# Weaving the first layer's attention with its projection, and taking slabs into the delta stage

## The chip, the cores and the metric

The kernel runs on one core of one Trainium2 chip. It is a single launch that holds its whole activation state in SBUF and streams all weights from HBM. The metric is the device time of that core in microseconds (us): the kernel before takes 2646.89 us, the median of three runs (2643.5 to 2648.5).

## The reference

Two transformer blocks run one after the other on 512 tokens of width 1024, all in fp32:

```python
def reference(...):
    x = first_block(x, mem, ...)        # two layers
    return second_block(x, meta, ...)   # two layers, 16 meta tokens ahead: 528 tokens

# first_block, layer i
h = rmsnorm(x, norm_mix[i]); mkv = rmsnorm(mem) @ w_mem_kv[i]
# i = 0: 12 query heads on 4 key heads, window of 128 either side, ALiBi bias, sink logit
# i = 1: 12 heads, neighbourhood of 8 x 16 on a grid of width 64, learned bias
y_tok = windowed_gqa(...) if i == 0 else neighbourhood_attn(...)
y_mem = memory_attn(qm, mk, mv)         # 4 heads, dense on 256 memory tokens, no bias
x = x + concat(y_tok, y_mem) @ w_out[i]
x = x + (silu(g) * u) @ w_down[i]       # g, u = rmsnorm(x) @ w_gate_up[i]

# second_block, layer 0: even_mixer
a_gate_in, a_gate_out, a_h, qkv, z, beta, alpha = split(h @ w_in)
y_a = a_gate_out * causal_dwconv(a_gate_in * a_h)
q, k, v = split(silu(causal_dwconv(qkv)))       # q and k are l2-normed, 4 heads of 128
o = gated_delta_rule(q, k, v, sigmoid(beta), g(alpha))   # chunks; state 128 x 128 a head
y_b = rms_norm(o, dn_norm_w) * silu(z)          # by head, over its 128 features
x = x + concat(y_a, y_b) @ w_out
# then a convolutional FFN; layer 1: sliding-window attention with sinks, and its FFN
```

## The kernel before

**Numbers and weights.** An fp32 product is made of three: each operand is split into a rounded half "hi" and the rest "lo", and TensorE adds hi x hi, hi x lo and lo x hi. Activations lie with features on the partitions, eight tiles of 128 features by 528 tokens. Weights come as slabs of 128 output features with all 1024 inputs (`UP`). A ring of two slots s = 0, 1 holds them: SyncE loads `raw` when GpSimd has ended the split before (`load_slabs`, `stream`), ScalarE rounds it to `w_hi` in two halves of 512 columns (`split_hi`, L987), GpSimd makes `w_lo` (`split_lo`, L695), TensorE multiplies (`many`, L1466: 24 products for 512 tokens, 48 where 528 tokens are taken as two times 264), and VectorE evicts PSUM and frees slot and accumulator (`acc_free[s]`). The pair q of slots is counted through the whole program.

**The order.** `plan()` lists the stages. Every engine walks them with its own in-order program; semaphores tie the five programs together. Nothing is reordered at run time, so an instruction that waits holds up all behind it on its engine.

**First layer.** `proj(10, 2, 1)` makes all twelve slabs (eight of queries, two of keys, two of values) before its attention. The attention goes by pairs: one block of 128 queries of two heads. There are 24 window pairs (six tiles of two heads, four blocks, 256 keys at the edges and 384 inside) and eight memory pairs. For a pair TensorE makes scores (L1591), VectorE adds the bias and takes maxima (L2013, L2008), ScalarE the exponentials, TensorE turns the probabilities (L1604), ScalarE copies them back, TensorE multiplies the values (L1660) and spreads the inverse sums (L1675), ScalarE and VectorE keep and normalise (`spread`, `move_y`, `invert`, `normalise`); GpSimd splits queries, keys and outputs. Eight output slabs (`out`) follow.

**Second layer.** Its attention is woven already: `proj(2, 6, 1)`, and then one list of 32 pairs, eight of memory and 24 of the neighbourhood (`woven_row`). On TensorE each pair's turn is

```python
scores(p)
if p.back(2).exists:
    transpose(p.back(2))
woven_part(p)
if p.back(3).exists:
    values(p.back(3))
```

with `woven_part` half a slab (L1694): six pairs of slabs, query and key tile of two heads, in rows 0 to 23, and from row 24 on output tiles by `OUT_PARTS`. An entry (s, k) there is slab s, feature tile k; a half of a slab's tiles needs that half of its split. GpSimd's `attend_woven` interleaves `prepare` (the splits of queries, keys and values and the bias mask, four "chores" a pair of heads) with the half splits and the outputs' splits; before its first chore it waits for both accumulators of the projection.

**Even stage.** 28 slabs; the last four make the gate that multiplies the convolved branch `conv_y`, evicted on VectorE at the end of `even`. While they run, ScalarE and VectorE end the l2 norms and the gates of the delta rule.

**Delta stage.** Chunks of 16, 128, 128, 128 and 128 tokens go through a software pipeline: rounds -1 to 5 of six pieces each (`rounds`, `PIECES`). In a round one chunk is prepared (`new`, `pre`), one has its triangular matrix inverted by up to six levels of doubling (`here`, `first_product` L1830 and `second_products`, with masked matrices `a_lv` from GpSimd, L917), and one runs through the state (`old`, `tail`: value of the keys, turned keys, new values, output, state; `tail` 0 to 4). `gated_split` on GpSimd splits the gated branch tile by tile in rounds 1 to 4. After the last round `tile_norm` normalises the four heads over all 528 tokens (squares on ScalarE, sums by products with ones L1811, root, VectorE, rounding L1359, GpSimd's `head_split` L910). Only then do the eight output slabs begin: TensorE waits for `gated_lo` and `head_lo`.

Of the kernel before, what the change touches and what calls it, by code (L numbers as in the profile page):

```python
# [17 lines left out]
P = 128  # L18
# [62 lines left out]
def plan():  # L81
# [84 lines left out]
    slabs(28, UP)  # L166
# [3 lines left out]
    add("tn", what="head", n=4)  # L170
    c["tn"] += 4
# [22 lines left out]
def delta_steps():  # L194
# [7 lines left out]

    for c, (_, n) in enumerate(CHUNKS):
# [4 lines left out]
        for part, engines in (("pre", pre), ("tail", tail)):  # L208
# [14 lines left out]
def build(nc, d):  # L223
# [6 lines left out]
    with ctx:  # L230
# [125 lines left out]
        neg_ident = small("neg_ident", [P, P])  # L356
        dn_cst = small("dn_cst", [P, d["dn_consts"].shape[1]], f32, 12416)
# [50 lines left out]
        split_acc = acc(2, 2)  # L408

# [112 lines left out]

        class Pair:
# [63 lines left out]
        def woven_rest(st):  # L587
# [4 lines left out]
        OUT_PARTS = {24: [(0, 6), (0, 7)], 25: [(0, 0), (0, 1)], 26: [(0, 2)], 27: [(1, 6), (1, 7)], 28: [(1, 0)],  # L592
                     29: [(1, 1)], 30: [(1, 2)], 31: [(0, 3)]}
# [12 lines left out]
        def _(sp):  # L606
# [50 lines left out]
            for n, st in enumerate(stages):  # L657
# [9 lines left out]
                if st.kind == "att" and st.woven:  # L667
# [4 lines left out]
                    for i in range(st.nt):  # L672
                        stream(st.slab0 + 4 + 2 * i)
                        if i + 2 < st.nt:
                            load_bias(st, i + 2)
# [13 lines left out]
        def _(pool):  # L689
# [27 lines left out]
            def prepare(st):  # L717
# [26 lines left out]
                def stage_k(i):  # L744
# [15 lines left out]
                    elif st.woven:  # L760
                        src, kt = ring_tiles(st, i)[1], t
# [50 lines left out]
            def attend_woven(a):  # L812
# [4 lines left out]
                for s in range(RING):  # L817
                    pool.wait_ge(acc_free[s], first)
# [4 lines left out]
                for p in row:  # L823
                    u, n = p.at // 4, p.at % 4
                    if p.at + 4 < len(row):
                        then = row[p.at + 4]
                        if then.st is b and n < 2:
                            pool.wait_ge(acc_free[n], first + then.tile + 1)
                        chores[then.st][n](then.tile)
                    if n < 2 and 1 <= u <= W_TILES:  # L830
                        split_lo(first + u, 1, UP, (n,))
                    if n >= 2 and u < W_TILES:
                        split_lo(first + u + 1, 0, UP, (n - 2,))
# [4 lines left out]
                streamed(2 * (first + W_TILES) + 2)  # L838
# [59 lines left out]
            def gated_split(st, m):  # L898

                for s in range(RING):  # L900
                    pool.wait_ge(acc_free[s], st.slab0 // 2)
# [5 lines left out]
            def head_split(st):  # L907
                for j in range(4):
                    pool.wait_ge(head_hi, j + 1)
                    nc.gpsimd.tensor_tensor(h_lo[st.h][:, 4 + j, :], normed_o[:, j % 2, :],  # L910
                                            h_hi[st.h][:, 4 + j, :].bitcast(f32), ALU.subtract).then_inc(head_lo, 1)

            def delta(st):

                pool.wait_ge(loaded, 16 * N_LOADS + 16)
# [6 lines left out]
                for here, mid, old, new, i in rounds():  # L922
# [33 lines left out]
                stream(st.slab0 + 2)  # L956

            for n, st in enumerate(stages):
# [3 lines left out]
                if st.kind == "tn" and st.what == "head":  # L962
                    head_split(st)
# [13 lines left out]
        def _(act):  # L977
# [98 lines left out]
            def attend(st):  # L1076
                off = 1 if st.sink is None else 0

                def probs(p, h):
# [3 lines left out]
                    s_h = s_sb[0:p.nq, p.slot, h, off:p.n + 1]  # L1083
# [56 lines left out]
                def spread(p):  # L1140

                    if st.summed:
                        return
                    act.wait_ge(inv_ready, p.kept + 1)
# [6 lines left out]
                def move_y(p):  # L1151
                    if st.summed:
# [39 lines left out]
                def turned_woven(p):  # L1192
                    act.wait_ge(pt_done, 2 * p.count + 2)
                    act.wait_ge(pv_done, p.count - 1)
# [3 lines left out]
                def split_woven(p):  # L1198
                    first, u, n = st.slab0 // 2, p.at // 4, p.at % 4
                    if n < 2 and 1 <= u <= W_TILES:  # L1200
                        split_hi(first + u, 1, UP, (n,))
                    if n >= 2 and u < W_TILES:
# [1447 lines left out]
```

## Time and profile before

| | us |
|---|---|
| median of three runs | 2646.89 |
| the profiled execution, its own time | 2646.34 |
| its span from first to last instruction | 2644.6 |
| TensorE busy in the span | 2541.5 |
| TensorE loading weights | 2196.2 |
| GpSimd / VectorE / ScalarE busy | 1201.3 / 959.7 / 919.9 |
| mean granted TensorE clock, of full speed | 0.981 |

Times in the trace count from the start of the span. A line Lnnn is a line of the kernel; helpers share one line, so a group is told apart by its tiles (`w_lo<-raw,w_hi`). A duration of a group "x12" runs from the first instruction to the end of the last. Idle time in brackets stands before the instruction, with what ended it. The granted clock is the mean over a stretch: 1.0 is 2.4 GHz, 0.5 is 1.2 GHz.

### The profile page before, as it was taken

What the parts mean: (1) busy time and instruction counts of PE and PEld (TensorE: products, weight loads), DVE (VectorE), ACT (ScalarE), POOL (GpSimd) and SP (SyncE); (2) the same over time, 40 slices, a digit from 0 to 9 for tenths busy, and PEclk for the clock granted to TensorE, in tenths of its full rate; (3) what the DMA queues carried; (4) which work ended last, traced back from release to release, by engine and by line L of the source; (5) the groups of instructions that cost most, each with busy time, mean ns of one, the idle gap of its engine ahead of it and who ended that gap; (6) DMA issues with size and microseconds to landing.
All of it is one profiled execution on the core that took longest, in us unless ns stands there. A gap on an engine that the chain in (4) does not pass through costs nothing.

```text
span 2644.6 us, 46681 instructions
## 1 busy us (share of the span) xinstructions
PE 2541.5 (96%) x16758; PEld 2196.2 (83%) x16758; DVE 959.7 (36%) x1748; ACT 919.9 (35%) x1988; POOL 1201.3 (45%) x1039
## 2 busy tenths in 40 slices
PE   7999999999999999999998979999999888999999
PEld 7767888888776888888997869999999667998897
DVE  4263221223445221226753433422432543441341
ACT  4284322232244322234242223322233565322231
POOL 4554444444565444444442534444444443444443
PEclk9999999999999999999998989999999999999999
DMA  5211232232121222232221002232222100223222
GB/s 174 80 42 64 95 103 87 91 106 83 53 63 58 92 95 99 87 107 88 83 77 41 2 20 93 87 101 78 92 93 75 33 25 33 90 93 99 92 93 97
DMA packets 59473, 209.16 MB, mean 79 GB/s; under 512 B 8544, under 2 KB 11232, under 8 KB 59360
## 3 DMA queue, kind: packets, MB, share of 16 engines
q1 hardware_dynamic: 59360, 207.66, 24.1%
q8 instruction: 70, 1.15, 0.2%
q14 instruction: 43, 0.35, 0.0%
HBM read 205.54 MB, written 2.10 MB: 79 GB/s over the span
## 4 chain that ended last, share of the span: by engine, by line
PE 90%; DVE 4%; ACT 2%; issue 2%; POOL 1%; SPq 1%; DVEq 0%; DMA 0%; ACTq 0%; POOLq 0%
PE ps L1466 74%; PE ps L1694 3%; PE ps L1660 2%; PE ps L1642 1%; PE ps L1830 1%; PE ps L1591 1%; PE ps L1619 1%; PE ps L1819 1%; DVE s_sb L2013 1%; PE ps L1481 1%; PE ps L1669 1%; PE ps L1684 1%; DVE y_sb L1988 0%; DVE s_sb L1988 0%; PE ps L1604 0%
## 5 line engine op out<-in xcount | busy, mean ns | idle before, releaser
L695 POOL TENSOR_TENSOR w_lo<-raw,w_hi 128x512 fp32r<-128x512 f32 (+1 forms) x704 | 977.4, 1409 | 1156.1 <-ACT w_hi L987 1155.7
L987 ACT ACTIVATE w_hi<-raw 128x512 fp32r<-128x512 f32 (+1 forms) x704 | 428.2, 653 | 1276.0 <-PE ps L1466 1256.5
L1466 PE MATMUL ps<-h_hi,w_hi 128*128 128x264 f32 (+2 forms) x2832 | 791.4, 329 | 11.4 <-POOL h_lo L910 8.0
L1466 PE MATMUL ps<-h_lo,w_hi 128*128 128x264 f32 (+2 forms) x2832 | 789.5, 328 | 0.0
L1466 PE MATMUL ps<-h_hi,w_lo 128*128 128x264 f32 (+2 forms) x2832 | 786.8, 328 | 0.0
L1466 PEld LDWEIGHTS ps<-h_hi,w_hi 128*128 128x128 f32 x2832 | 479.8, 189 | 64.9 <-issue 13.8
L1466 PEld LDWEIGHTS ps<-h_lo,w_hi 128*128 128x128 f32 x2832 | 476.5, 189 | 48.1 <-issue 1.0
L1466 PEld LDWEIGHTS ps<-h_hi,w_lo 128*128 128x128 f32 x2832 | 476.7, 189 | 47.2
L1466 PE MATMUL ps<-act_lo,w_hi 128*128 128x512 f32 (+1 forms) x880 | 280.5, 351 | 0.0
L1466 PE MATMUL ps<-act_hi,w_lo 128*128 128x512 f32 (+1 forms) x880 | 279.8, 350 | 0.0
L1466 PE MATMUL ps<-act_hi,w_hi 128*128 128x512 f32 (+1 forms) x880 | 278.8, 349 | 0.0
L1988 DVE TENSOR_TENSOR x<-x,ps 128x512 f32<-128x512 f32 (+3 forms) x96 | 66.6, 693 | 432.0 <-PE ps L1466 430.5
L1466 PEld LDWEIGHTS ps<-act_hi,w_hi 128*128 128x128 f32 x880 | 153.3, 188 | 24.4
L1466 PEld LDWEIGHTS ps<-act_lo,w_hi 128*128 128x128 f32 x880 | 153.6, 188 | 24.0
L1466 PEld LDWEIGHTS ps<-act_hi,w_lo 128*128 128x128 f32 x880 | 153.9, 188 | 22.7
L1988 DVE TENSOR_TENSOR ps<-gated,ps 128x512 f32<-128x512 f32 (+1 forms) x88 | 61.6, 701 | 169.4 <-PE ps L1466 169.1
L1983 DVE SCALAR_TENSOR_TENSOR ps<-padded,vec,ps 128x528 f32<-128x528 f32 (+1 forms) x132 | 101.2, 767 | 25.9 <-issue 15.5
L1988 DVE TENSOR_TENSOR act_lo<-ps,act_hi 128x512 f32 (+1 forms) x88 | 61.2, 696 | 104.3 <-ACT act_hi L1252 104.3
L1988 DVE TENSOR_TENSOR padded<-ps,rstd 128x528 f32<-128x528 f32 (+1 forms) x56 | 39.4, 703 | 154.8 <-PE ps L1466 143.6
L1983 DVE SCALAR_TENSOR_TENSOR h_lo<-x,vec,h_hi 128x512 fp32r<-128x512 f32 (+2 forms) x64 | 59.4, 928 | 81.2 <-ACT h_hi L994 68.1
L1249 ACT ACTIVATE ps<-ps 128x512 f32<-128x512 f32 (+1 forms) x88 | 51.5, 585 | 105.8 <-DVE ps L1983 105.8
L1988 DVE TENSOR_TENSOR gated<-ps,rstd 128x512 f32<-128x512 f32 (+1 forms) x88 | 61.2, 696 | 73.2 <-ACT ps L1249 73.2
(311 smaller groups left out, 2785.0 us busy)
## 6 DMA issues: line engine op xcount, KB each, us to landing
raw<-slabs_d SPq DMA_DIRECT2D x288, 512.0 KB, 3.3
raw<-slabs_d SPq DMA_DIRECT2D x64, 704.0 KB, 4.0
bias_sb<-alibi_d SPq DMA_DIRECT2D x6, 384.0 KB, 3.7
x<-x_d SPq DMA_DIRECT2D x1, 2048.0 KB, 13.5
out_d<-x SPq DMA_DIRECT2D x8, 256.0 KB, 4.4
rpb_raw<-rpb_d SPq DMA_DIRECT2D x6, 256.0 KB, 2.7
mem_in<-mem_d SPq DMA_DIRECT2D x1, 1024.0 KB, 7.2
cst<-consts_d SPq DMA_DIRECT2D x1, 792.0 KB, 9.4
```

What stands on the lines that cost most here:

```text
L695: nc.gpsimd.tensor_tensor(w_lo[:, s, a * P:b * P], raw[:, s, a * P:b * P], w_hi[:, s, a * P:b * P].bitcast(f32), ALU.subtract).then_inc(lo ...
L987: nc.scalar.activation(w_hi[:, s, a * P:b * P], raw[:, s, a * P:b * P], ACT.Copy)\
L1249: nc.scalar.activation(acc(2, st.used), acc(2, st.used), ACT.Silu).then_inc(silu_ready, 1)
L1466: last = nc.tensor.matmul(ps[:, s * 2 * BANK + po:s * 2 * BANK + po + n], w[:, s, wk], columns(a, k, to, n), start=(k == 0 and w is w_hi a ...
L1481: last = nc.tensor.matmul(out, a[:, k, t0:t0 + n], w[:, s, wk], start=(k == 0 and w is w_hi and a is hi), stop=(k == DT - 1 and w is w_lo))
L1591: last = nc.tensor.matmul(p.score(h)[0:p.nq, col:col + n], a[hp, p.tile_slot, p.q], b[hp, p.tile_slot, k0:k0 + n], start=(b is k_hi and a ...
L1619: last = nc.tensor.transpose(to, s_sb[0:p.nq, p.slot, h, 1 + col:1 + col + n], ident[0:p.nq, 0:p.nq])
L1642: last = nc.tensor.matmul(split_acc[:, c, :], wt[:, w.s, k * P:(k + 1) * P], a[:, k, to:to + n], start=(k == 0 and wt is w_hi and a is hi) ...
L1660: nc.tensor.matmul(out[HD * h:HD * h + HD, 0:p.nq], v_st[0:n, p.tile_slot, vb, HD * h:HD * h + HD], p_t[0:n, p.slot, h, j, 0:p.nq], start= ...
L1694: last = nc.tensor.matmul(acc(s, 1), w[:, s, k * P:(k + 1) * P], columns(a, k, META, SEQ), start=(k == first and w is w_hi and a is hi), s ...
L1983: return nc.vector.scalar_tensor_tensor(*a, **kw)
L1988: return nc.vector.tensor_tensor(*a, **kw)
```

## The change

Three stages take part. **First layer:** it is woven as the second. Its projection keeps two memory query slabs and two value slabs; the memory pairs come first; eight slabs stand in the list: two key-and-query pairs in halves (rows 0 to 7), then, since three query heads share a key head, four query slabs in quarters (rows 8 to 23), all of them in one accumulator; the other accumulator serves the turned probabilities of window pairs, which need a bank more. Output tiles stand in rows 24 to 31 (`OUT_FIRST`). `spread`, `move_y` and `invert` join the woven lists of ScalarE and VectorE.

**Shared by both woven layers:** GpSimd's chores begin when the first accumulator is free, and the second layer's output tiles go in the order 0, 1, 2, 6, 7 with two rows between the slab's halves.

**Delta stage:** the four gate slabs leave the even stage for pieces 0 to 11 of the delta stage, a third of a slab each (`GATE_PARTS`), with their splits in pieces 3 to 13 (`GATE_SPLITS`), which also split the first halves and second halves of two output slabs. The head norm goes chunk by chunk two rounds behind (`mean_o`, `square_o`, `root_o`, `norm_o`, `head_round`, `head_split`). The last chunk's turned keys and state update go (`ends`). Quarters and halves of the first two output slabs are put into the last round and behind it (`out_part`). The host lays the first layer's weights out in the new order.

```diff
-    proj(10, 2, 1)
-    out[-1].queries = (0, 1, 2, 4)
+    proj(2, 2, 1)
+    out[-1].queries = (0,)
+    out[-1].woven = True
+    att(nt=2, blocks=m_blocks, bias=None, sink=None, qt=0, kt=0, group=1, y=6, layer=0)
+    out[-1].woven = True
+    slabs(2 * 2, UP)
     att(nt=6, blocks=a_blocks, bias="alibi", sink=0, qt=0, kt=6, group=3, y=0, layer=0)
-    att(nt=2, blocks=m_blocks, bias=None, sink=None, qt=8, kt=0, group=1, y=6, layer=0)
-    tail(2, 1, 0, False, (3, 1))
+    out[-1].woven = True
+    slabs(4, UP)
+    tail(2, 1, 0, False, (3, 1), woven=True)
...
-    slabs(28, UP)
+    slabs(24, UP)
     add("delta", pre=norms[-1])
-    add("tn", what="head", n=4)
+    slabs(4, UP)
...
+    ends = dict(pe=["vks", "vn", "o"], dve=["res"], act=["vn", "o"], pool=["ke", "qe"])
...
+        GATE_PARTS, GATE_SPLITS = 12, {3: (1, 0, 0), 4: (1, 0, 1), 6: (1, 1, 0), 7: (1, 1, 1), 9: (2, 0, 0),
+                                       10: (2, 0, 1), 12: (2, 1, 0), 13: (2, 1, 1)}
...
-        OUT_PARTS = {24: [(0, 6), (0, 7)], 25: [(0, 0), (0, 1)], 26: [(0, 2)], 27: [(1, 6), (1, 7)], 28: [(1, 0)],
-                     29: [(1, 1)], 30: [(1, 2)], 31: [(0, 3)]}
+        OUT_FIRST = {24: [(0, 0)], 25: [(0, 1)], 26: [(0, 2)], 27: [(0, 6)], 28: [(0, 7)], 31: [(0, 3)]}
+        def woven_slab(a, p):
+            first, u, n = a.slab0 // 2, p.at // 4, p.at % 4
+            if u >= W_TILES:
+                return None
+            if u < 2 or not shares_keys(a):
+                return first + u, n // 2, range(n % 2 * DT // 2, (n % 2 + 1) * DT // 2), n // 2
+            return first + 2 + (u - 2) // 2, u % 2, range(n * DT // 4, (n + 1) * DT // 4), 0
...
+        OUT_PARTS = {24: [(0, 0), (0, 1)], 25: [(0, 2)], 26: [(0, 6), (0, 7)], 27: [(1, 0), (1, 1)], 28: [(1, 2)],
+                     29: [(1, 6)], 30: [(1, 7)], 31: [(0, 3)]}
...
-                for s in range(RING):
-                    pool.wait_ge(acc_free[s], first)
+                pool.wait_ge(acc_free[0], first)
                 for n in (0, 1, 2):
                     chores[a][n](0)
...
+                        if then.st is a and n == 0:
+                            pool.wait_ge(acc_free[1], first)
...
+                    if e in GATE_SPLITS:
+                        pair, s, part = GATE_SPLITS[e]
+                        split_lo(st.slab0 // 2 + pair, s, UP, (part,))
+                    if past_o and i == 5:
+                        head_split(st, past_o)
...
                         probs(p, 1)
+                        if p.back(1).exists:
+                            spread(p.back(1))
+                        if p.back(2).exists:
+                            move_y(p.back(2))
                         if p.back(3).exists:
                             y_hi(p.back(3))
                         split_woven(p)
...
+                def gate_part(t):
+                    m, part = divmod(t, 3)
+                    q, s = st.slab0 // 2 + m // 2, m % 2
+                    if part == 0:
+                        begin(q, s)
+                        pe.wait_ge(acc_free[1 - s], q + s)
...
-                for here, _, old, new, i in rounds():
+                for here, _, old, new, i, e, past_o in parts():
+                    if e < GATE_PARTS:
+                        gate_part(e)
                     if here:
                         first_product(here, here.levels[i])
...
+                    if past_o and i == 1:
+                        mean_o(past_o)
+                    if old and old.c == LAST.c and i == 2:
+                        LAST.after(pe, "pre", "dve", "qk")
+                        LAST.after(pe, "pre", "act", "off")
+                        out_part(0, range(0, 2))
+                out_part(0, range(2, 4))
+                mean_o(LAST)
+                LAST.after(pe, "tail", "act", "o")
+                out_part(1, range(0, 4))
+                for s in range(RING):
+                    out_part(s, range(4, DT))
```

## Rows read from the trace of the kernel before

**Rows 1.** The page, parts 1 and 4: busy time by engine, chain by engine.
```profile
PE 2541.5 (96%) x16758; PEld 2196.2 (83%) x16758; DVE 959.7 (36%) x1748; ACT 919.9 (35%) x1988; POOL 1201.3 (45%) x1039
...
PE 90%; DVE 4%; ACT 2%; issue 2%; POOL 1%; SPq 1%; DVEq 0%; DMA 0%; ACTq 0%; POOLq 0%
```

**Rows 2.** Windows: length, PE, PEld, DVE, ACT, POOL busy, clock, DMA, GB/s.
```profile
121.38:209.57 88.19, 78.45 (x736) 55.69 (x737) 60.48 (x193) 70.61 (x257) 44.66 (x69) 0.94 0.11 34
1423.00:1445.26 22.26, 11.90 (x124) 10.30 (x124) 8.24 (x25) 7.12 (x20) 6.80 (x15) 0.61 0.00 1
1445.26:1470.50 25.24, 22.75 (x338) 19.42 (x339) 10.65 (x23) 7.20 (x18) 12.14 (x14) 0.91 0.01 2
1470.50:1541.20 70.70, 61.84 (x984) 55.58 (x985) 31.41 (x62) 18.76 (x45) 34.91 (x37) 0.93 0.02 7
1541.20:1572.48 31.28, 15.31 (x69) 12.66 (x69) 11.04 (x13) 10.94 (x18) 5.69 (x5) 0.72 0.07 21
```

**Rows 3.** Chain of waits, first layer: start, us, what (eight and nine slabs).
```profile
76.06 44.52 PE ps L1466 x192
...
209.57 51.73 PE ps L1466 x216
```

**Rows 4.** Chain of waits, second layer, woven rows.
```profile
677.74 5.49 PE ps L1694 x12
...
739.84 0.59 PE ps L1660 x8
740.42 0.44 PE ps L1669 x8
...
742.00 2.78 PE ps L1694 x12
```

**Rows 5.** Timeline of TensorE, first layer: start, us, operation.
```profile
150.08 0.91 PE L1604 MATMUL ps<-cst,s_sb 128*128 128x128 f32 x6
...
152.70 0.65 PE L1604 MATMUL ps<-cst,s_sb 128*128 128x128 f32 x4
```

**Rows 6.** Timeline of VectorE and GpSimd, start of the second layer's woven list.
```profile
672.99 1.27 DVE L1998 COPY val_w<-ps 128x384 f32<-128x384 f32 x3
...
673.02 0.61 POOL L723 CAST q_hi<-ring 128x512 fp32r<-128x512 f32 x1 [9.73 <-issue]
```

**Rows 7.** Timeline of GpSimd and TensorE, second layer, row 24 and end.
```profile
800.84 1.26 POOL L695 TENSOR_TENSOR w_lo<-raw,w_hi 128x512 fp32r<-128x512 f32 x1 [0.37 <-ACT w_hi L987]
...
802.36 0.70 PE L1694 MATMUL ps<-y_w,w_hi 128*128 128x512 f32 x2 [3.41 <-POOL w_lo L695]
...
841.50 0.73 PE L1466 MATMUL ps<-y_w,w_hi 128*128 128x512 f32 x2 [1.43 <-POOL w_lo L695]
```

**Rows 8.** Chain of waits, the four gate slabs of the even stage.
```profile
1399.46 23.47 PE ps L1466 x192
```

**Rows 9.** Timeline of VectorE, ScalarE and TensorE, start of the delta stage.
```profile
1404.48 0.18 DVE L1983 SCALAR_TENSOR_TENSOR gate<-dn_s,ea 128x20 f32<-128x20 f32 x1 [0.44 <-issue]
...
1423.01 1.15 ACT L987 ACTIVATE w_hi<-raw 128x512 fp32r<-128x512 f32 x2 [4.72 <-PE ps L1466]
...
1445.26 1.12 PE L1830 MATMUL ps<-x_m,a_lv 64*64 64x64 f32 x16 [3.16 <-POOL a_lv L917]
```

**Rows 10.** Timeline of four engines, end of the delta stage.
```profile
1545.77 1.89 PE L1819 MATMUL ps<-res,x_full 128*128 128x128 f32 x8
...
1564.47 0.70 ACT L1352 ACTIVATE root<-ps,vec 128x528 f32<-128x528 f32 x1 [1.06 <-PE ps L1811]
...
1568.07 1.34 POOL L910 TENSOR_TENSOR h_lo<-normed_o,h_hi 128x528 fp32r<-128x528 f32 x1 [6.72 <-ACT h_hi L1359]
...
1586.97 0.70 DVE L1988 TENSOR_TENSOR x<-x,ps 128x528 f32<-128x528 f32 x1 [2.43 <-PE ps L1466]
```

**Rows 11.** Timeline of VectorE: the state's update in two rounds.
```profile
1493.96 0.96 DVE L1988 TENSOR_TENSOR state<-state,erow 128x512 f32<-128x512 f32 x1
...
1550.43 0.69 DVE L1988 TENSOR_TENSOR state<-state,erow 128x512 f32<-128x512 f32 x1 [3.87 <-PE ps L1891]
```

More of the change, by code:

```diff
@@ L207, in delta_steps @@
                    pool=["em", "xm", "first", "xt"])
-        for part, engines in (("pre", pre), ("tail", tail)):
+        for part, engines in (("pre", pre), ("tail", tail if c + 1 < len(CHUNKS) else ends)):
             for engine, names in engines.items():
@@ L356, in build @@
         neg_ident = small("neg_ident", [P, P])
+        o_sq = small("o_sq", four)
         dn_cst = small("dn_cst", [P, d["dn_consts"].shape[1]], f32, 12416)
@@ L521, in rounds, with parts @@
                     yield here, mid, old, new, i
+        def parts():
+            for e, (here, mid, old, new, i) in enumerate(rounds()):
+                r = e // PIECES - 1
+                yield here, mid, old, new, i, e, Chunk(r - 2) if r >= 2 else None
+        GATE_PARTS, GATE_SPLITS = 12, {3: (1, 0, 0), 4: (1, 0, 1), 6: (1, 1, 0), 7: (1, 1, 1), 9: (2, 0, 0),
+                                       10: (2, 0, 1), 12: (2, 1, 0), 13: (2, 1, 1)}
+        LAST = Chunk(len(CHUNKS) - 1)
         class Pair:
@@ L826, in attend_woven @@
                         then = row[p.at + 4]
+                        if then.st is a and n == 0:
+                            pool.wait_ge(acc_free[1], first)
                         if then.st is b and n < 2:
-                            pool.wait_ge(acc_free[n], first + then.tile + 1)
+                            if then.tile < 2 or not shares_keys(a):
+                                pool.wait_ge(acc_free[n], first + then.tile + 1)
+                            elif n == 0:
+                                pool.wait_ge(acc_free[then.tile % 2], first + 2 + (then.tile - 2) // 2 + 1)
                         chores[then.st][n](then.tile)
[L830 to L833, printed above, removed]
+                    for q, s, part in woven_splits(a, p):
+                        split_lo(q, s, UP, (part,))
                     if p.back(3).exists:
@@ L920, in all_heads @@
                     return m[0:n, 0:w].unsqueeze(1).to_broadcast([n, DN_H, w])
-                for here, mid, old, new, i in rounds():
+                for here, mid, old, new, i, e, past_o in parts():
                     if here:
@@ L1140, in spread @@
                 def spread(p):
-                    if st.summed:
+                    if p.st.summed:
                         return
+                    if p.row and p.back(2).exists and p.back(2).st.summed:
+                        act.wait_ge(y_ready, p.count - 1)
                     act.wait_ge(inv_ready, p.kept + 1)
@@ L1198, in split_woven @@
                 def split_woven(p):
[L1199 to L1202, printed above, removed]
-                        split_hi(first + u + 1, 0, UP, (n - 2,))
+                    for q, s, part in woven_splits(st, p):
+                        split_hi(q, s, UP, (part,))
                 if st.woven:
@@ L1215, in attend @@
                     turned_woven(last)
-                    for k in (2, 1, 0):
-                        y_hi(last.back(k))
+                    spread(last)
+                    move_y(last.back(1))
+                    y_hi(last.back(2))
+                    move_y(last)
+                    y_hi(last.back(1))
+                    y_hi(last)
                     return
@@ L1418, in delta @@
                         pre(new, i)
+                    if e in GATE_SPLITS:
+                        pair, s, part = GATE_SPLITS[e]
+                        split_hi(st.slab0 // 2 + pair, s, UP, (part,))
+                    if past_o and i == 0:
+                        square_o(past_o)
+                    if past_o and i == 2:
+                        root_o(past_o)
+                    if past_o and i == 4:
+                        head_round(past_o)
+                square_o(LAST)
+                root_o(LAST)
+                head_round(LAST)
             for st in stages:
@@ L1841, in first_product @@
                     k.after(pe, "levels", "pool", ("am", s))
+                    if s == k.levels[0] and k.c == 0:
+                        pe.wait_ge(gate_made, 2)
                     if s == k.levels[0]:
@@ L1920, in delta @@
                     pe.wait_ge(acc_free[s], st.slab0 // 2)
-                for here, _, old, new, i in rounds():
+                for here, _, old, new, i, e, past_o in parts():
+                    if e < GATE_PARTS:
+                        gate_part(e)
                     if here:
@@ L2503, in delta @@
                     fill(x_fulls[e][SIDE:P, :, 0:SIDE], 0.0).then_inc(gate_made, 1)
-                for here, _, old, new, i in rounds():
+                for here, _, old, new, i, e, past_o in parts():
                     if here:
```

236 lines of the change are left out of this document (169 added, 67 removed).

## The prediction

> **What bounds the kernel now.** I read the page's first and fourth parts, then stages by windows, then chain and timeline around each edit. TensorE is busy for 2541.5 of 2644.6 us and holds 90% of the chain that ended last [rows 1]. A gain must therefore come from the few stretches where TensorE waits or works at the lower of its two clocks: the attention of the first layer (78.45 us busy in 88.19), the first two rounds of the delta stage (11.90 in 22.26, mean granted clock 0.61) and its end with the norm of the heads (15.31 in 31.28) [rows 2].
>
> **Terms.** The profiled execution took 2646.34 us (span 2644.6); the median of the runs is 2646.89, so a difference found in the trace is taken from 2646.5. I follow three stretches from one fixed point to another, and call a saving negative.
>
> **A, first layer: from the end of its fourth slab (76.06) to the end of the second output slab.** Before: eight slabs take 44.52, so one is 5.57; the attention ends where the output begins, at 209.57; nine slabs take 51.73 there, 1.6 more than 9 x 5.57 since they start at the low clock [rows 3]. Two of them end at 209.57 + 11.1 + 1.6 = 222.3, which makes 146.2.
> After: the same ten slabs, 55.7, stand between the parts of the 32 pairs on TensorE. A pair of the memory kind costs TensorE 742.00 - 739.84 = 2.16 [rows 4]. A window pair with 384 keys costs 2.62: that is one turn of the loop, from transposes at 150.08 to the next transposes at 152.70 [rows 5], an upper bound, since TensorE partly waited there. With 256 keys it is a memory pair without its eight products for the sums (0.44 [rows 4]) and with one product of 128 columns more, some 0.3: 2.0. Eight by 2.16 and 24 by 2.3 is 72.5; with the slabs 128.2. What doesn't hide:
> - the start. The last copy of the values ends 1.8 us after the projection in the second layer [rows 6], and TensorE waits for it: 1.9; the first half slab then took 5.49 where later ones take 2.78 [rows 4]: 2.7.
> - the weights' splits. ScalarE puts its half of the rounding behind the moving of the output of the pair before, which comes only when TensorE has ended the next row. From there 0.3 for the move, 0.3 for the rounded output, 0.6 for w_hi (1.15 for two [rows 9]) and 1.26 for w_lo [rows 7] are 2.5; TensorE has 1.4 until it wants the slab (scores and transposes of one row). 1.1 at each of the four slabs in rows 12 to 27: 4.4.
> - the last eight rows, of 2.3 plus one output tile (0.7), which is less than the handover of a row needs: 2. The first slab after them waits 1.4, as at 841.50 [rows 7].
> Sum 140.6, so A = -5.6. Below it lies -14 (no wait but the start), above it +2 (a wait of 1.1 in most rows, and window pairs that cost 2.62 all). Hidden at no cost are VectorE's evictions (one a slab) and GpSimd's chores, since a row lasts 2.3 and a quarter slab, 3.7 us. SyncE's queue has now slab loads between the ALiBi loads; each is asked for when GpSimd has split the slab before it in that buffer, two slabs or some eight rows ahead of its use. If that cover went, a row would wait for a load's landing, a few us once.
>
> **B, second layer, which shares the code.** GpSimd's chores now wait for one accumulator, not two: before, it slept 9.73 and began at 673.02 [rows 6], although the tile that it needs comes from the slab before the last, one slab (5.57) earlier. Its chores of 3.4 us (673.02 to 676.46, where its split begins [rows 6]) end by 672.99 then, and TensorE goes on when the values are kept (672.99 + 1.27 [rows 6]), with scores at 674.4 and the slab at 675.0 instead of 677.74 [rows 4]: -2.7. Row 24 of this stage asked for both halves of an output slab and stood 3.41 [rows 7]; the second half came at 802.10 (800.84 + 1.26), since GpSimd masks the next bias ahead of it. In the new order only the first half is needed there, which was split 4 us earlier, and the second two rows later: -3.4, and -1.5 for the slower products behind the wait. With 0.3 at row 27, B = -7.9. If the shorter wait also keeps the clock up, 2.7 more; if another input is late in row 24, -4 remains.
>
> **C, delta stage: from 1399.46 to the end of the second output slab (1586.97 [rows 10]).**
> C1, rounds -1 and 0 with the gate slabs. Before: slabs 23.47 [rows 8] and rounds to the first product of round 1 at 1445.26 [rows 9], 45.8 in all. After: the slabs, in twelve parts (2.2, 2.2, 1.5), 23.5; the rounds' own products, 11.90 at a clock of 0.61 [rows 2], are 7.3 at the high clock. Then the waits, in TensorE's order. The gate is ready only at 1404.66 [rows 9], formerly hidden by the slabs; only the first part (to 1401.7) stands ahead of it, and one copy for ScalarE follows: 3.4. Every new slab uses the same accumulator and waits for VectorE's eviction: 0.7, 0.9, and 2.6 for the fourth, since that eviction stands behind four operations on 128 tokens. GpSimd has the split of a half slab in front of the masked matrices of the next piece, and that split waits for ScalarE, which waits for the round's exponentials: 2.0 in round 0; before round 1 the split (1.26 for 512 columns [rows 7], so some 0.7 for 256) stands ahead of the masked matrices, of 256 columns each: 2.5 with ScalarE's share. Handovers inside three levels: 1.3. That is 13.4 of waits. They also drop the clock, as the 22.26 before: about 5 (two stretches like A's 2.7). Sum 49.2: +3.4. Bounds: -11 (all but the gate's wait hidden, no low clock) and +8.
> C2, round 1: the two last half splits stand before the masked matrices of levels two and three. Masked matrix, split and ScalarE's half come one after the other: 0.7 + 1.3 + 0.6, against TensorE's 2 us of work: +4; bounds 0 and +7.
> C3, rounds 2 to 4 (70.70 [rows 2]): two mean products over 512 columns, at 1.0 to 1.9 each, by the eight products of 128 columns at 1545.77 [rows 10]; 0.6 a round for the queues: +4; bounds +1 and +8.
> C4, the end. Before, from 1541.20 to 1586.97: 45.8. After: first tail product 3.7 (4.57 to 1545.77 less the transposes that go, 0.8), mean 1.1, next product 1.8 [rows 10], a quarter slab 1.5 while ScalarE copies, products of the output 1.9, a quarter slab 1.5, mean 1.1, half of slab two 2.9. Then the last heads: from root to split 1564.47 to 1569.41, 4.9 [rows 10], of which 2.9 are covered: 2.2 with handover. The remaining halves 5.9. Sum 23.6: -22; bounds -25 and -17.
> C = 3.4 + 4 + 4 - 22 = -10.6.
>
> A rule bears on C3. VectorE's state update took 0.96 beside a running GpSimd instruction and 0.69 without [rows 11]; the sum takes such 0.3. The Trainium skill, "SBUF — State Buffer", section "SBUF: two separate sides", says that a VectorE operation with two SBUF inputs and GpSimd lock one port pair, the later blocked for a whole instruction. By it each of the ten norm operations could wait up to 1.3, 13 us in the worst case; this trace shows a fifth of that.
>
> **Sum.** -5.6 - 7.9 - 10.6 = -24: 2646.5 - 24.1 = 2622.4, told as 2622.
>
> **Rivals.**
> 1. The slabs hide. C1 and C2 at their lower bounds (-11 and 0) and A at -9 give 2622 - 14.4 - 4 - 3.4 = 2600. For it: TensorE had 10 us idle there. Against: the splits stand in the queue of GpSimd, on which round 1 waited 3.16 already [rows 9]. 0.16.
> 2. The delta stage gives nothing: C1 at +8, C2 and C3 at +6, C4 at -18 make +2, and A is -3: 2646.5 + 2 - 3 - 7.9 = 2638. For it: each added operation stands in a queue that a level waits for. Against: in rounds 2 to 4 TensorE is the busy engine (61.84 of 70.70, VectorE 31.41, GpSimd 34.91 [rows 2]). 0.13.
> 3. Slower: the clock. The gate slabs were a dense run that left the clock high; in pieces they might never raise it. If all of 1399 to the end of round 4 ran at the low clock, the 23.5 + 7.3 + some 80 of products in rounds 1 to 4 (22.75 at 0.91 and 61.84 at 0.93 are 78 [rows 2]) would cost as much again, 109, of which rounds fill idle time with 10. It decides from 30 us on, that is from two rounds wholly low; at three rounds (+45): 2622 + 45 = 2667. For it: rounds -1 and 0 did run at 0.5 to 0.6. Against: round 1 came back by itself, to a mean of 0.91. 0.06.
> 4. Weaving does nothing for layer one, A at 0 to +2 since TensorE was 89% busy there; the rest as forecast: 2629. It lies in the forecast's own range.
>
> **How the numbers follow.** The forecast has 0.65, with its own range 2611 to 2633. The range to hold eight in ten reaches into rivals 1 and 2: 2603 to 2638. A measurement of this kernel tells 0.2% (5.3 us) from no change. Faster: 0.65 + 0.16 + 0.13, less 0.04 for the ends of the forecast and of rival 2 that touch that bound, is 0.90; same 0.04 and 0.01 of rival 3; slower 0.05.
>
> **What would show it.** Right: no wait over 0.5 at row 24 of the second layer, GpSimd's first chore there near 667; the first product of round 1 some 49 us after the last pair slab, with waits for GpSimd's masked matrices before rounds 0 and 1; the first two output slabs done 24 us after round 4. Wrong: round 1 at 1435 on the old clock axis (rival 1), a granted clock under 0.7 in rounds 1 to 4 (rival 3), or window rows in the first layer of 4.5 us instead of 3.8 (A too small).

## The result and the profile after

The changed kernel takes 2620.16 us (median of five runs, 2619.66 to 2629.81) against 2647.86 (2643.5 to 2648.5): ratio 0.9904, interval 0.9891 to 0.9917. Forecast were 2622 and faster. The profiled execution took 2620.16 us (span 2618.4), 26.2 less than the one of before. The page, parts 1 and 4, answers to [rows 1]; TensorE is busy for 12 us less with nearly the same number of products:

```profile
PE 2529.4 (97%) x16740; PEld 2183.0 (83%) x16740; DVE 970.3 (37%) x1755; ACT 921.4 (35%) x1984; POOL 1201.1 (46%) x1040
...
PE 92%; DVE 3%; ACT 2%; issue 2%; POOL 1%; DMA 0%; DVEq 0%; SPq 0%; ACTq 0%; POOLq 0%
```

Windows of the kernel before, cut where the prediction cut (columns as in [rows 2]): A, B, rounds -1 and 0, rounds 2 to 4, the delta stage's end, and, new here, the stretch from the second block's first FFN slab to its second attention's output.

```profile
76.06:222.35 146.29, 135.73 (x977) 101.74 (x977) 69.12 (x206) 82.48 (x278) 72.28 (x92) 0.95 0.15 49
672.17:841.50 169.33, 158.40 (x1173) 116.02 (x1171) 82.54 (x195) 69.43 (x158) 103.98 (x120) 0.97 0.17 52
1399.46:1445.26 45.80, 35.35 (x316) 33.54 (x315) 14.91 (x37) 12.17 (x29) 14.33 (x21) 0.81 0.11 35
1470.50:1541.23 70.73, 61.84 (x985) 55.61 (x985) 31.41 (x62) 18.76 (x45) 34.94 (x37) 0.93 0.02 8
1541.23:1586.94 45.71, 29.77 (x166) 27.09 (x167) 13.22 (x16) 13.22 (x22) 8.69 (x7) 0.75 0.07 20
1628.91:2221.18 592.27, 567.19 (x4647) 530.69 (x4646) 224.80 (x494) 228.97 (x591) 256.30 (x248) 0.98 0.22 70
```

The same stretches of the changed kernel, with round 1 as the fourth row (25.24 before [rows 2]):

```profile
78.02:217.23 139.21, 130.39 (x980) 94.97 (x978) 77.37 (x213) 83.22 (x270) 67.83 (x88) 1.00 0.17 55
666.91:824.66 157.75, 153.67 (x1174) 112.97 (x1172) 82.52 (x195) 69.68 (x158) 99.18 (x114) 1.00 0.17 56
1382.83:1435.15 52.32, 39.67 (x317) 37.26 (x317) 15.02 (x37) 11.02 (x27) 17.38 (x22) 0.84 0.12 40
1435.15:1468.73 33.58, 27.22 (x339) 22.84 (x339) 10.66 (x23) 8.35 (x20) 14.51 (x16) 0.76 0.05 18
1468.73:1543.18 74.45, 63.80 (x990) 56.31 (x991) 38.15 (x68) 24.96 (x58) 33.56 (x36) 0.95 0.01 2
1543.18:1565.96 22.78, 20.35 (x142) 18.73 (x143) 5.72 (x9) 7.67 (x13) 4.68 (x4) 0.93 0.01 1
1607.93:2195.22 587.29, 563.21 (x4648) 527.17 (x4646) 224.55 (x494) 228.91 (x591) 256.42 (x248) 0.99 0.21 70
```

Read in pairs, the first column gives this account:

| term | forecast | measured |
|---|---|---|
| A, first layer | -5.6 | -7.1 |
| B, second layer | -7.9 | -11.6 |
| C1, rounds -1 and 0 | +3.4 | +6.5 |
| C2, round 1 | +4 | +8.3 |
| C3, rounds 2 to 4 | +4 | +3.7 |
| C4, end of the delta stage | -22 | -22.9 |
| FFN and last attention, not edited | 0 | -5.0 |
| start up to the fourth slab, not edited | 0 | +2.0 |

That is 26.1 of the 26.2 us by which the two profiled executions differ. The total came out right in part by luck, since errors cancelled: the delta stage gave 4.4 instead of 10.6, and B, A and a stage that no edit touches made up for it.

### The profile page after: what moved, and what is told of

Read it like the earlier page. It is cut to its first block, busy times and chain, and to the rows that moved or that the text cites. A ratio compares the mean times of both kernels' runs of the same rounds, so it can differ in the third digit from the quotient of the medians.

```text
span 2618.4 us, 46299 instructions
## 1 busy us (share of the span) xinstructions
PE 2529.4 (97%) x16740; PEld 2183.0 (83%) x16740; DVE 970.3 (37%) x1755; ACT 921.4 (35%) x1984; POOL 1201.1 (46%) x1040
## 3 DMA queue, kind: packets, MB, share of 16 engines
q1 hardware_dynamic: 59360, 207.66, 23.7%
## 4 chain that ended last, share of the span: by engine, by line
PE 92%; DVE 3%; ACT 2%; issue 2%; POOL 1%; DMA 0%; DVEq 0%; SPq 0%; ACTq 0%; POOLq 0%
PE ps L1568 72%; PE ps L1802 5%; PE ps L1762 2%; PE ps L1693 1%; PE ps L1793 1%; PE ps L1744 1%; PE ps L1984 1%; PE ps L1721 1%; PE ps L1583 1%; PE ps L1943 1%; PE ps L1973 1%; PE ps L1771 1%; POOL w_lo L751 0%; PE ps L1777 0%; PE ps L1961 0%
## 5 line engine op out<-in xcount | busy, mean ns | idle before, releaser
L1568 PE MATMUL ps<-h_hi,w_hi 128*128 128x264 f32 (+2 forms) x2608 | 718.8, 326 | 0.1
L1568 PE MATMUL ps<-h_lo,w_hi 128*128 128x264 f32 (+2 forms) x2608 | 717.3, 326 | 0.0
L1568 PE MATMUL ps<-h_hi,w_lo 128*128 128x264 f32 (+2 forms) x2608 | 715.6, 325 | 0.0
L1568 PEld LDWEIGHTS ps<-h_hi,w_hi 128*128 128x128 f32 x2608 | 439.6, 188 | 47.1 <-issue 1.6
L1568 PEld LDWEIGHTS ps<-h_hi,w_lo 128*128 128x128 f32 x2608 | 436.5, 188 | 41.6
L1568 PEld LDWEIGHTS ps<-h_lo,w_hi 128*128 128x128 f32 x2608 | 435.9, 188 | 42.3 <-issue 1.0
L1568 PEld LDWEIGHTS ps<-act_hi,w_lo 128*128 128x128 f32 x880 | 153.9, 188 | 22.7
```

Source lines behind the costliest of these rows:

```text
L1568: last = nc.tensor.matmul(ps[:, s * 2 * BANK + po:s * 2 * BANK + po + n], w[:, s, wk], columns(a, k, to, n), start=(k == 0 and w is w_hi a ...
```

## Experiments

Each was timed beside the kernel before on the same chip. Most read a stretch of the trace, because the time also swings in stages that the edit doesn't reach.

**c_only and ab_only: one part alone.** c_only has the edits of the delta stage and of its place in `plan()` and the even stage, ab_only all others.

> The kernel before with the delta stage's part of the change alone. Theory, from the two traces: the delta stage, from the start of the gate slabs to the end of the second output slab, is worth -4.5 us (+6.5 in rounds -1 and 0, +8.3 in round 1, +2.0 in rounds 2 to 4, -21.4 at the end), so some 2643 against 2647.9. Rival, the terms of the prediction: -10.6, so 2637. In the trace: the stretch from the first gate slab to the third output slab is 183.0 by the theory, 177 by the rival, 187.4 before.

> The kernel before with the woven first layer and the code it shares with the second, without the delta stage's part. Theory, from the two traces: -7.2 in the first layer and -11.6 in the second, 18.8 together, so some 2629 against 2647.9. Rival, the terms of the prediction: -5.6 and -7.9, so 2634. In the trace the woven second layer, from the end of its projection to its third output slab, is 157.7 by the theory and 161.4 by the rival.

c_only took 2641.6 (ratio 0.9967, 0.9954 to 0.998), ab_only 2646.24 (0.9991, 0.9981 to 1.0001), which is nearly nothing. Windows of c_only, round 1 and the last stretch, then of ab_only, the woven second layer, the last stretch and round 1:

```profile
1452.68:1486.27 33.59, 27.23 (x338) 22.79 (x339) 10.66 (x23) 8.35 (x20) 14.51 (x16) 0.76 0.05 17
1629.31:2219.35 590.04, 566.30 (x4648) 530.20 (x4646) 225.00 (x494) 228.84 (x591) 256.38 (x248) 0.98 0.21 70
```

```profile
665.27:824.53 159.26, 155.16 (x1174) 114.14 (x1172) 82.48 (x195) 69.67 (x158) 98.97 (x114) 0.99 0.18 56
1616.96:2222.60 605.64, 583.68 (x4646) 540.82 (x4646) 224.71 (x494) 228.89 (x591) 256.08 (x248) 0.95 0.21 68
1428.66:1458.24 29.58, 27.23 (x339) 23.25 (x339) 10.67 (x23) 7.19 (x18) 12.01 (x14) 0.73 0.01 2
```

Round 1 of c_only is the 33.6 of the changed kernel. The median lies near the theory's 2643, but the profiled execution (2644.53) doesn't show its -4.5: the whole delta stage, from 1399.99 to 1587.33, takes 187.34 there for the 187.48 of before. In ab_only the first layer's 139.2 and the second's 159.3 are there, 17 us less than before, and they are lost again where no edit is: 13.4 in the last attention stage, at a mean clock of 0.95 for 0.98, and 4.3 in round 1, at 0.73 for 0.91. The profiled execution is the longest of the eleven (2650.07). Theory and rival both missed the total of ab_only; of its stretches the first layer is as in the changed kernel, and the second lies between theory and rival (157.7 and 161.4), nearer the theory. By the totals the parts do not add up: 6.3 and 1.7 us alone, 27.7 together.

**ab_later: the same kernel, the last attention begun later.**

```diff
-                for po, to, n in chunks(nm.blk):
+                for po, to, n in chunks(nm.blk) * (5 if nm.gain == 8 else 1):
```

> The kernel with the two woven layers and the delta stage of before (ab_only), and eight more products of 264 columns in the sum of squares ahead of the last attention stage: that stage begins 1.8 us later, all else is the same. Theory: no edit of the two layers reaches that stage; it stays at the low clock for some 40 us at its end or not by when it begins, so begun at another time most executions take 587 to 592 there and the median falls to about 2635. Rival: something in the kernel itself (another state of buffers or of loads) keeps it low; the stage stays at 605 and the median at 2648.

Measured: 2634.16 (nine runs from 2628.7 to 2648.28), ratio 0.9964 (0.9946 to 0.9981): with eight products more it is some 10 us faster than ab_only, if the 1.8 by which the kernel before differed between the two are taken off. The added products cost 3.6 us, twice what was expected. The sum of squares in ab_only and in ab_later, on the chain of waits:

```profile
2002.98 0.89 PE ps L1545 x4
```

```profile
2000.45 4.45 PE ps L1545 x20
```

The last 41.5 us of that attention stage in ab_only, in ab_later and in the changed kernel:

```profile
2181.10:2222.60 41.50, 38.08 (x184) 25.83 (x183) 8.75 (x40) 15.59 (x61) 5.04 (x10) 0.50 0.04 13
```

```profile
2167.70:2209.20 41.50, 35.53 (x249) 24.49 (x250) 14.61 (x62) 22.77 (x89) 10.46 (x19) 0.79 0.05 14
```

```profile
2153.70:2195.20 41.50, 34.45 (x280) 23.87 (x281) 16.54 (x70) 26.73 (x102) 13.44 (x24) 0.92 0.07 22
```

In the same time TensorE issued 184, 249 and 280 products. So the loss doesn't come with the woven layers as such, which are the same in both: the rival, 605 and 2648, falls. The median is the theory's, though the delay was twice the one that it reckoned with. The profiled execution took 594.78 from FFN to output, 591.2 without the added products, and the runs still scatter over 20 us, one of them at 2648.28. Whether the later begin or the denser run of products ahead of the stage does it, this run doesn't tell apart.

**late_splits: C2.** The four half splits of the output slabs go from pieces 9 to 13 to rounds 3 and 4.

```diff
-GATE_SPLITS = {..., 9: (2, 0, 0), 10: (2, 0, 1), 12: (2, 1, 0), 13: (2, 1, 1)}
+GATE_SPLITS = {..., 25: (2, 0, 0), 27: (2, 0, 1), 31: (2, 1, 0), 33: (2, 1, 1)}
```

> The changed kernel with the four half splits of the first two output slabs moved from the last pieces of round 0 and the first of round 1 to rounds 3 and 4; the gate slabs stay in pieces. Theory: the splits stand in GpSimd's queue ahead of the masked matrices of levels one and two, and the waits (4.68 and 0.61) with the low clock behind them are the 8.3 that round 1 lost: 2612, round 1 in some 26 us. Rival: round 1 is long because the pieces ahead of it leave the clock low; it stays over 30 us, and the time at 2618.

Measured: 2615.02 (ratio 0.9875, 0.986 to 0.9889). Rounds 1 and 3, and round 3 of the changed kernel:

```profile
1431.15:1456.64 25.49, 22.45 (x339) 19.43 (x339) 11.37 (x24) 7.20 (x18) 11.76 (x14) 0.93 0.01 1
...
1482.46:1512.82 30.36, 24.49 (x341) 21.45 (x341) 15.90 (x26) 10.35 (x23) 16.01 (x17) 0.89 0.06 19
```

```profile
1494.81:1520.66 25.85, 21.52 (x341) 18.71 (x341) 14.38 (x26) 9.31 (x21) 13.12 (x15) 1.00 0.01 2
```

Round 1 is back from 33.58 to 25.49: the theory holds for the round and the rival (over 30) falls; the total is 3 us above the theory's 2612. Round 3, where two of the splits now stand, takes 30.36 for the 25.85 of the changed kernel. TensorE's idle time there is 5.87 for 4.33, so 1.5 of the 4.5 are waits; the other 3.0 are the same products at a granted clock of 0.89 for 1.00.

**gates_back: C1.** `slabs(28, UP)` in the even stage again, no gate parts, splits of the output slabs at pieces 25, 27, 31 and 33.

> The changed kernel with the four gate slabs back in the even stage; norms by chunks and early output slabs stay, and the output slabs' splits stand in rounds 3 and 4. Theory: the gate slabs in pieces cost 6.5 in rounds -1 and 0 and 8.3 in round 1, and both go: 2620.2 - 14.8 = 2605. Rival 1: TensorE's idle time in rounds -1 and 0, 10 of 22.3 us, was filled by the pieces, and the time returns: 2620 or more. Rival 2: the low clock of those rounds comes back in full and only round 1 is won: 2612.

Measured: 2615.22 (ratio 0.9885, 0.9871 to 0.9899), between the two rivals, with 6.2 us less in the delta stage than the changed kernel in the profile. It differs from late_splits by the place of the gate slabs alone, and its time is the same. Rounds -1 and 0 are at their old length, as the theory had it, and round 1 takes 27.5; round 3 takes 29.8, and the total stays 10 us above the theory's 2605. GpSimd in gates_back, round 3:

```profile
1491.15 1.26 POOL L749 TENSOR_TENSOR w_lo<-raw,w_hi 128x512 fp32r<-128x512 f32 x1 [10.96 <-ACT w_hi L1046]
1492.38 0.73 POOL L972 TENSOR_TENSOR a_lv<-a_t,dn_cst 128x256 f32<-128x256 f32 x1
```

GpSimd stands for 10.96 us for ScalarE's rounding, with the next level's masked matrix (`a_lv`) queued behind. What that cost TensorE is less than it looks: it was idle for 5.30 us in the round, 1.0 more than in the changed kernel, and busy for 24.49, 3.0 more, at a clock of 0.89.

**apart: the two engines' halves told apart.**

```diff
+GATE_SPLITS = {30: (0, 0, 0), 31: (0, 0, 1), 32: (0, 1, 0), 33: (0, 1, 1)}   # ScalarE alone
...
+                    if e == 35:
+                        for s in range(RING):
+                            split_lo(st.slab0 // 2, s, UP)
```

> The kernel with the gate slabs back in the even stage, and the output slabs' splits told apart by engine: ScalarE's four roundings in the pieces of round 4, GpSimd's four subtractions together at the end of round 4. Theory: GpSimd stood 10.96 and 6.55 for ScalarE's rounding with the masked matrices of the next level behind it, so that round 3 took 29.8 where it takes 25.0 in the kernel before; with the halves apart round 3 takes 25.5, round 4 a us less, and the time is 2610 (2615 less 5). Rival: what made round 3 longer is the norm by chunks on VectorE and the port it shares with GpSimd; round 3 stays at 29 and the time at 2615.

Measured: 2611.93 (2609.82 to 2634.13), ratio 0.9858 (0.9844 to 0.9873). Rounds 3 and 4, and then the first piece of round 3 in apart and in the changed kernel:

```profile
1485.74:1514.16 28.42, 24.34 (x340) 21.41 (x340) 14.37 (x26) 9.31 (x21) 13.08 (x15) 0.89 0.01 2
1514.16:1535.12 20.96, 17.84 (x311) 15.35 (x311) 10.56 (x18) 9.27 (x19) 10.55 (x11) 1.00 0.01 2
```

```profile
1485.74:1493.49 7.75, 7.75 (x74) 7.32 (x74) 2.04 (x4) 0.38 (x1) 0.76 (x2) 0.59 0.01 2
```

```profile
1494.81:1499.94 5.13, 4.92 (x74) 4.61 (x74) 2.01 (x4) 0.38 (x1) 0.77 (x2) 1.00 0.01 3
```

Round 4 fell from 23.7 to 21.0 and the end from 24.6 to 22.7, but round 3 only to 28.4, so the time lies between theory and rival. The theory's waits did go: TensorE's idle time in round 3 is 4.08 for the 5.30 of gates_back. What keeps the round 2.6 us longer than in the changed kernel is its first piece alone, 7.75 for 5.13 with the same 74 products, at a clock of 0.59 for 1.00. No split of the output slabs stands in this round, and the norm by chunks, the rival's cause, is the same in both kernels: the rival falls too. The profiled execution is the longest of the five (2634.13), in which the last attention stage again took 606.88; in best1, which has the same delta stage, rounds 3 and 4 took 27.46 and 23.55. So the gain of the two rounds together on gates_back is 4.1 in the one profile and 2.4 in the other.

**act_first: the waits of A.**

```diff
                         probs(p, 1)
+                        split_woven(p)
                         if p.back(1).exists:
                             spread(p.back(1))
...
                             y_hi(p.back(3))
-                        split_woven(p)
```

> The changed kernel with ScalarE's half of the weights' split moved, in the woven lists, from the end of a row to right behind the second exponential, ahead of the moving and the rounding of outputs. Theory: ScalarE waits in each row for TensorE's values of the row after, and the slab's rounding stood behind that; the waits for w_lo at the four slabs in rows 12 to 27 of the first layer (1.07 the first, then as much) go: -4.5 there, from 139.2 to 134.7. Rival: the slab's load or GpSimd's own queue is what is late, and at most 1 us goes. The second layer stays at 157.7 by both.

Measured: 2613.74 (ratio 0.9889, 0.9863 to 0.9914), and 133.29 for the first layer's stretch. Timeline of TensorE in the changed kernel, the four waits of rows 12 to 27, none of which is left in act_first:

```profile
132.52 0.50 PE L1802 MATMUL ps<-h_hi,w_hi 128*128 128x512 f32 x1 [1.07 <-POOL w_lo L751]
148.61 0.50 PE L1802 MATMUL ps<-h_hi,w_hi 128*128 128x512 f32 x1 [1.08 <-POOL w_lo L751]
164.68 0.50 PE L1802 MATMUL ps<-h_hi,w_hi 128*128 128x512 f32 x1 [1.08 <-POOL w_lo L751]
180.76 0.73 PE L1802 MATMUL ps<-y_w,w_hi 128*128 128x512 f32 x2 [1.08 <-POOL w_lo L751]
```

```profile
77.44:210.73 133.29, 129.63 (x982) 94.98 (x979) 69.67 (x213) 83.80 (x270) 67.98 (x88) 1.00 0.18 57
```

The cause is the order of ScalarE's queue; the rival falls. The gain is 5.9, more than the four waits (4.3); some 1.0 of the rest lies in the last eight rows, and it was not resolved. The second layer was not read in this run; in best1, which has the same order, it took 157.71.

**chores_late and old_order: B in two.** The first makes GpSimd wait for both accumulators again, the second gives back the old `OUT_PARTS`.

```diff
                 pool.wait_ge(acc_free[0], first)
+                if not shares_keys(a):
+                    pool.wait_ge(acc_free[1], first)
```

> The changed kernel with GpSimd waiting again for both accumulators before the first chore of the second layer. Theory: the first half slab then begins 2.8 later and, behind the longer wait, runs at the low clock (5.5 for 3.0): +5.3 in the stretch from the end of the second layer's projection to its third output slab, 163.0 for 157.7. Rival, the prediction's figure: +2.7, with the clock unchanged: 160.4.

> The changed kernel with the second layer's output tiles in the order of before (tiles 6 and 7 first, so that row 24 needs both halves of the slab's split). Theory: what is left of the second layer's 11.6 when the chores' 5.3 are taken off, +6.3, so 164.0 for 157.7. Rival, the prediction's terms for row 24 and row 27: +5.2, 162.9. If the order is worth nothing: 157.7.

Measured: 163.23 and 164.55 for 157.75 (times 2624.34 and 2629.55, ratios 0.9906 and 0.9932), both near their theories. The first half slab on the chain of chores_late and of the changed kernel, and TensorE of old_order at row 24:

```profile
673.57 5.49 PE ps L1804 x12
```

```profile
669.68 3.00 PE ps L1802 x12
```

```profile
790.55 1.19 PE L1802 MATMUL ps<-y_w,w_hi 128*128 128x512 f32 x2 [3.42 <-POOL w_lo L751]
```

The 5.5 of the first are a later begin and a first half slab of 5.49 where the changed kernel has 3.00; the prediction's -2.7 had left that out. The 6.8 of the second begin with the old wait, 3.42 for the 3.41 of [rows 7]. 5.5 + 6.8 is 12.3, about B's 11.6.

**best1 and pieces_apart: what to keep.** best1 is apart with act_first's order; pieces_apart has the same two edits and the gate slabs in pieces.

> Gate slabs back in the even stage, the output slabs' splits told apart by engine, and ScalarE's rounding of the weights ahead of the moving of outputs in the woven lists: the three edits that gained by themselves. Theory: they lie in different stages and add up: first layer 133.3, delta stage 315.4, so 2611.9 less 5.9 = 2606 where the last attention stage takes its 587, and some 18 more in an execution where it stays at the low clock. Rival: the earlier start moves the delta stage to another place against the clock and half is lost: 2610 to 2612.

> As the changed kernel with the gate slabs in pieces, with the output slabs' splits told apart by engine in round 4 and ScalarE's rounding ahead in the woven lists. Theory: against the same kernel with the gate slabs in the even stage it loses the 4.3 of rounds -1 and 0 (3.4 of it the wait for the gate), and wins up to 2 in round 1: 2 to 4 us slower than that one, 2608 to 2610. Rival: with the splits out of the way the pieces fill TensorE's idle time and it is the faster: under 2604.

best1 took 2605.64 (2603.35 to 2609.61), ratio 0.985 (0.9836 to 0.9865): it beats both kernels. That the edits add up is told by the stretches and not by the total, whose interval holds the rival's 2610 too once the kernel before, 2.6 us faster beside best1 than beside apart, is allowed for: the first layer took 133.32, and the delta stage 188.2 for the 187.4 of apart. pieces_apart took 2617.6, its six runs in two groups, 2606.1 to 2608.2 and 2627.0 to 2631.2. In its profile, of the first group, the delta stage is 1.6 us shorter than in best1: what the pieces lose ahead of round 1 (+3.0) they win in it (24.0 for 27.8, at a clock of 0.97 for 0.81). So neither side of that expectation holds. In these two profiles it hardly matters where the gate slabs stand once the splits are out of the way. But the median of pieces_apart is 12 us above that of best1, and no profile fell in its second group: whether the pieces bring that group about is not shown.

## Why the prediction was right, and where it was not

**A** (-5.6, measured -7.1). Its waits stand in the trace as they were worked out: 1.1 at each of four slabs is 1.07 to 1.08, 1.4 at the first slab behind the rows is 1.45. Too large was the start: the first half slab took 2.97, not 5.49, and the granted clock of the whole stretch was 1.00. The first half slab, and the first output slab behind the rows:

```profile
80.21 2.97 PE ps L1802 x12
```

```profile
217.23 0.73 PE L1568 MATMUL ps<-y_w,w_hi 128*128 128x512 f32 x2 [1.45 <-POOL w_lo L751]
```

This is 2.5 of error the one way; elsewhere the stretch cost about a us more than worked out, and where was not traced.

**B** (-7.9, measured -11.6). The term for the start was mis-sized here too: "if the shorter wait also keeps the clock up, 2.7 more" was named and left out of the sum, and it came (5.49 to 3.00). The wait at row 24 went as forecast, and came back with the old order.

**C1** (+3.4, measured +6.5). The step that failed is not the waits. TensorE's timeline of the changed kernel:

```profile
1388.38 1.88 PE L1973 MATMUL ps<-cst,gb 16*128 16x16 f32 x8 [3.13 <-ACT gb L1457]
...
1397.52 0.48 PE L1943 MATMUL ps<-h_hi,w_hi 128*128 128x264 f32 x2 [0.59 <-DVE conv_y L2160]
...
1404.86 0.48 PE L1943 MATMUL ps<-h_hi,w_hi 128*128 128x264 f32 x2 [0.89 <-DVE conv_y L2160]
...
1413.79 0.36 PE L1984 MATMUL ps<-x_m,a_lv 16*16 16x16 f32 x8 [1.86 <-POOL a_lv L976]
...
1424.05 0.78 PE L1943 MATMUL ps<-h_hi,w_hi 128*128 128x264 f32 x2 [2.88 <-DVE conv_y L2160]
...
1435.15 0.68 PE L1984 MATMUL ps<-x_m,a_lv 64*64 64x64 f32 x16 [2.38 <-POOL a_lv L976]
...
1446.29 1.12 PE L1984 MATMUL ps<-x_m,a_lv 64*64 64x64 f32 x16 [4.68 <-POOL a_lv L976]
```

Forecast were 3.4, 0.7, 0.9, 2.0, 2.6 and 2.5 for the first six; 3.13, 0.59, 0.89, 1.86, 2.88 and 2.38 came, each with the releaser that was named. The term for the clock was mis-sized: 5 was taken, and TensorE was busy for 39.67 us where, by the prediction's own estimate, its products take 23.5 + 7.3 = 30.8 at the upper level, so 8.9. Part of the 6.5 belongs to the output slabs' splits in pieces 9 to 11: with these moved away (late_splits) the rounds were 2.5 shorter.

**C2** (+4, bounds 0 and +7, measured +8.3). The measured value lies outside the bounds, and the +4 was not derived: 0.7 + 1.3 + 0.6 against 2 us of work leaves 0.6 a level. Masked matrix, split and ScalarE's rounding did come one after the other. But ScalarE's rounding itself stood behind the next chunk's row of exponents, which waits for a product that TensorE issues after the level before. Rows of ScalarE and of GpSimd, round 1:

```profile
1443.00 0.60 ACT L1483 ACTIVATE erow<-ps 128x512 f32<-128x512 f32 x1 [6.75 <-DVE dlast L2160]
...
1443.59 0.62 ACT L1050 ACTIVATE w_hi<-raw 128x512 fp32r<-128x512 f32 x1
```

```profile
1444.29 1.26 POOL L751 TENSOR_TENSOR w_lo<-raw,w_hi 128x512 fp32r<-128x512 f32 x1 [9.20 <-ACT w_hi L1050]
1445.51 0.72 POOL L976 TENSOR_TENSOR a_lv<-a_t,dn_cst 128x256 f32<-128x256 f32 x1
```

So TensorE waited 4.68 at one level; and then the round ran at 0.76, so that the same products kept it busy for 27.22, 4.5 more than before. Wait (3.9 more of idle time) and clock each cost as much as the whole term; late_splits took both away. That the wait goes with the splits is shown: the five profiles with splits in round 1 took 33.1 to 33.6 there, and the eight without 24.0 to 29.6. That the low clock comes from the wait is not: in ab_only and apart, without a split in the round, the same products took 27.23 and 27.28.

**C3 and C4** (+4 and -22, measured +3.7 and -22.9). Right; the wait for the last heads' split was 2.17 for the 2.2 worked out. VectorE was busy for 6.7 us more in rounds 2 to 4 (38.15 for 31.41), and the rounds became 3.7 longer. Six of the ten norm operations stand in these rounds. The first operation of a norm over 128 tokens beside a running instruction of GpSimd, that instruction, and the same operation with GpSimd idle:

```profile
1536.81 1.44 DVE L2155 SCALAR_TENSOR_TENSOR qkv<-qkv,vec,o_sq 128x512 f32<-128x512 f32 x1
```

```profile
1536.44 1.27 POOL L976 TENSOR_TENSOR q_era<-qkv,erow 128x512 f32<-128x512 f32 x1
```

```profile
1549.06 0.75 DVE L2155 SCALAR_TENSOR_TENSOR qkv<-qkv,vec,o_sq 128x512 f32<-128x512 f32 x1 [3.12 <-ACT o_sq L1450]
```

The operation took 0.7 longer where GpSimd still ran for 0.9. The Trainium skill, "SBUF — State Buffer", section "SBUF: two separate sides", says that a VectorE operation with two SBUF inputs and a GpSimd instruction that reads SBUF lock one port pair, so that the later one waits for the whole of the other. The trace agrees in kind; the 0.7 is about half of the 1.3 that the prediction took as the worst case of one operation.

**Rivals.** 1 (slabs hide, 2600) failed, and not only at the splits that its "against" named: with these out of the way (pieces_apart) rounds -1 and 0 were still 2.7 longer than before. 3 (low clock in all rounds) did not come, though round 1 went part of that way. 2 (the delta stage gives nothing, +2) failed by the total, but what that stage did, -4.4, lies midway between it and the forecast, and the -0.1 of c_only is nearer to it.

**What no term held.** In 13 profiles the stretch from the FFN to the end of the last attention, unchanged but for eight products in ab_later, took between 587.07 and 606.88. The prediction's range held it by its width, not by an argument.

## What to carry to other kernels

When one engine's operation waits for another engine's, look at what stands in front of the second and behind the first: moving ScalarE's rounding ahead in its queue won 5.9 us here, nearly as much as the weaving of the first layer (7.1). Price a new wait twice, once for its length and once for the products behind it, which may run at the lower clock; in rounds -1 to 1 the second was about as large as the first. Judge an edit by its own stretch of the trace as well as by the total: 17 us that two stages gained were gone from the total of ab_only, in stages that it doesn't touch.

## What was not expected of the hardware

At the end of the last attention stage the granted clock can stay at its lower level (0.50, 1.2 GHz) for 41 us although TensorE is busy for 38.08 of 41.50 us, as in ab_only. In the changed kernel the same 184 products, the last of the stage, ran at the upper level:

```profile
2169.00:2195.20 26.20, 21.62 (x184) 15.13 (x185) 9.23 (x40) 15.88 (x62) 5.15 (x10) 1.00 0.07 21
```

From the FFN on, ten of the 13 profiles took 587 to 592 us, ab_later 595 (591 without its added products), and two 606, and but for these products no edit between them reaches the stage. What decides between the two outcomes stays open.
